# Expert loop of a hybrid-encoder kernel: each expert's turn and output products placed ahead of the next expert's up product

## The reference, cut to what matters

```python
def hier_moe(h, w_rg, b_rg, w_re, b_re, w1, w3, w2):
    ...  # combine: per token, weights of its two experts
    for gi in range(MOE_GROUPS):
        hid = silu(einsum('td,edf->tef', hf, w1[gi])) * einsum('td,edf->tef', hf, w3[gi])
        out = out + einsum('tef,efd->td', hid * combine[:, gi, :, None], w2[gi])
```

## Time and profile before

| | |
|---|---|
| median of 3 runs | 747.45 us (747.12 to 749.54) |
| the profiled execution | 747.47 us |
| its span, first to last instruction | 745.7 us |
| TensorE busy | 708.8 us (95%) |
| VectorE, ScalarE, GpSimd busy | 394.3, 266.3, 66.7 us |
| read from memory | 194.57 MB |
| granted TensorE clock, mean | 0.987 |

### The profile page before, as it was taken

The page is one execution under the profiler, slowest core; times in us unless marked ns, Lnnn a source line. Parts: engine busy times, 40 slices in busy tenths (PEclk is TensorE's granted clock), DMA queues, the critical chain, the costliest instruction groups (busy, mean ns, idle before and its releaser), DMA issues.

```text
span 745.7 us, 13196 instructions
## 1 busy us (share of the span) xinstructions
PE 708.8 (95%) x5610; PEld 568.5 (76%) x5610; DVE 394.3 (53%) x683; ACT 266.3 (36%) x378; POOL 66.7 (9%) x66
## 2 busy tenths in 40 slices
PE   9899999999999999999999999979999999988892
PEld 7689999978777777799998998866666666655442
DVE  3386867854555556997877457444422222121226
ACT  3246555446455254434436244332122112211001
POOL 0010000000000250530000000001111111111110
PEclk9999999999999999999999999999999999999997
DMA  9964756765765345333363467968999999999951
GB/s 367 416 228 170 281 182 221 278 225 213 266 249 218 130 163 172 117 114 115 114 226 121 162 226 285 422 272 321 420 415 420 419 421 420 418 421 419 419 235 56
DMA packets 30893, 200.48 MB, mean 269 GB/s; under 512 B 4999, under 2 KB 5383, under 8 KB 7410
## 3 DMA queue, kind: packets, MB, share of 16 engines
q1 hardware_dynamic: 27506, 193.01, 66.8%
q0 software_dynamic: 3328, 6.62, 2.4%
HBM read 194.57 MB, written 10.75 MB: 275 GB/s over the span
## 4 chain that ended last, share of the span: by engine, by line
PE 79%; DMA 10%; DVE 5%; ACT 2%; SPq 2%; issue 1%; DVEq 0%; ACTq 0%
PE ps L1421 77%; DMA ring<-in_expert_pieces 7%; DMA r_btm<-in_pieces 2%; SPq L420 1%; DVE ring_rounded L851 1%; PE ps L1541 1%; ACT ring_rounded L565 1%; PE ps L1828 1%; DMA ring<-in_pieces 1%; ACT r_lm L774 0%; DVE r_kq L1054 0%; DVE r_xs_rounded L1117 0%; DVE x_sb L1379 0%; DVE x_sb L1404 0%; DVE x_sb L1396 0%
## 5 line engine op out<-in xcount | busy, mean ns | idle before, releaser
L851 DVE TENSOR_TENSOR ring_rounded<-ring,ring_rounded 128x2048 fp32r<-128x2048 f32 x60 | 138.0, 2304 | 97.0 <-ACT ring_rounded L565 96.7
L1421 PE MATMUL ps<-hT_rounded,ring_rounded 128*128 128x256 f32 x832 | 154.6, 286 | 0.9 <-DVE x_sb_rounded L890 0.9
L565 ACT CAST ring_rounded<-ring 128x2048 fp32r<-128x2048 f32 x60 | 114.2, 1904 | 69.3 <-DMA ring<-in_pieces 39.7
L1421 PEld LDWEIGHTS ps<-hT_rounded,ring_rounded 128*128 128x128 f32 x832 | 131.6, 193 | 4.3 <-issue 4.2
L1421 PE MATMUL ps<-x_sb_rounded,ring_rounded 128*128 128x256 f32 x416 | 118.2, 284 | 0.0
L1421 PE MATMUL ps<-ring_rounded,hT_rounded 128*128 128x512 f32 x352 | 109.9, 393 | 0.0
L1421 PEld LDWEIGHTS ps<-x_sb_rounded,ring_rounded 128*128 128x128 f32 x416 | 80.3, 193 | 0.2 <-issue 0.2
L1421 PEld LDWEIGHTS ps<-ring_rounded,hT_rounded 128*128 128x128 f32 x352 | 65.3, 188 | 15.3 <-issue 2.2
L1421 PE MATMUL ps<-ring,r_lm 128*64 128x256 f32 x512 | 65.5, 380 | 3.2 <-DMA ring<-in_expert_pieces 3.2
L1421 PEld LDWEIGHTS ps<-ring,r_lm 128*64 128x64 f32 x512 | 42.8, 137 | 27.2 <-issue 12.5
L783 ACT ACTIVATE sq<-ps 128x128 f32<-128x128 f32 x32 | 8.9, 278 | 151.3 <-PE ps L1421 151.3
(11 more groups left out here) (298 smaller groups left out, 1106.0 us busy)
## 6 DMA issues: line engine op xcount, KB each, us to landing
ring<-in_pieces SPq DMA_DIRECT2D x76, 1024.0 KB, 5.1
ring<-in_expert_pieces SPq DMA_DIRECT2D x48, 1024.0 KB, 19.6
r_z<-in_expert_pieces SPq DMA_DIRECT2D x12, 1024.0 KB, 15.8
r_xs<-in_expert_pieces SPq DMA_DIRECT2D x12, 1024.0 KB, 17.2
g_sb<-in_expert_pieces SPq DMA_DIRECT2D x6, 1024.0 KB, 17.4
r_st<-in_expert_pieces SPq DMA_DIRECT2D x6, 1024.0 KB, 19.1
r_bt<-in_expert_pieces SPq DMA_DIRECT2D x6, 1024.0 KB, 22.7
hT<-in_expert_pieces SPq DMA_DIRECT2D x6, 1024.0 KB, 22.2
```

The costliest lines, as they stand in the source:

```text
L565: nc.scalar.copy(high_of(p_), slot_of(p_)).then_inc(hi_ok, 1)
L851: nc.vector.tensor_tensor(low_of(p_), slot_of(p_), high_of(p_).bitcast(F32), ALU.subtract).then_inc(lo_ok, 1)
L1421: return nc.tensor.matmul(o, l, r, start=start, stop=stop)
```

## The change

TensorE finishes an expert before it begins the up product of the next: up(e), select(e+5), turn(e), down(e). At e = 0 select(4) stands between up(0) and select(5). ScalarE's and VectorE's lists follow: `silu_of(e)` ahead of the rows of quarter e+5, `hidden(e)` ahead of `hidden_turned(e)`. The late experts' picks move from e = 27 to e = 28. The up product and the hidden rows of expert 29 move behind the loop. The instructions are the same ones.

```diff
 # ScalarE
             for m in range(5):
                 rows_of_quarter(m)
-            silu_of(0)
             for e in range(EARLY_E):
-                silu_of(e + 1)
+                silu_of(e)
                 if e + 5 < E:
                     rows_of_quarter(e + 5)
...
-            for e in range(EARLY_E + 1, E):
+            for e in range(EARLY_E, E):
                 silu_of(e)
...
 # VectorE
             rows_of_choices()
-            hidden(0)
             for e in range(EARLY_E):
                 if e % 4 == 2 and e // 4 + 2 < E // 4:
                     pick_quad(e // 4 + 2)
+                hidden(e)
                 hidden_turned(e)
-                hidden(e + 1)
-                if e == EARLY_E - 2:
+                if e == EARLY_E - 1:
                     picks_of_late_experts()
                 output(e)
...
+            hidden(EARLY_E)
             hidden_turned(EARLY_E)
             rows_of_late_experts()
             output(EARLY_E)
...
 # TensorE
             for m in range(4):
                 select_quarter(m)
-            up_of(0)
-            select_quarter(4)
...
             for e in range(EARLY_E):
-                up_of(e + 1)
-                turn_of(e)
+                up_of(e)
+                if e == 0:
+                    select_quarter(4)
                 if e + 5 < E:
                     select_quarter(e + 5)
+                turn_of(e)
                 down_of(e)
...
+            up_of(EARLY_E)
             turn_of(EARLY_E)
             late_rows_turned()
             down_of(EARLY_E)
```

## The result

The changed kernel takes 771.8 us (median of 4 runs, 769.28 to 773.84), the kernel before 748.35 us (4 runs, 747.12 to 749.54). The ratio is 1.0306, 95% interval 1.0275 to 1.0337: 3.1% slower. The forecast was 763.2 us, with a range of 759 to 769. The direction was right, the size was not: 23.5 us instead of 15.8. The time lies above the range, where the forecast had put 3 chances in a hundred.

The account below looks back on a forecast made before the run. TensorE bounds the loop's first half and the weight stream its second. Waits at experts 0 and 2 and turns of 7.50 us instead of 6.71, slack included, add 15.8 to 747.47: 763.2 us, range 759 to 769.

Parts of the forecast that it names:

- The bound: Expert loop: TensorE paces the first half, the weight stream the second, with 10.2 us of slack; afterwards TensorE's own waits.
- Rival A: Expert loop: the stream stays the bound and the new waits vanish in it, 748.1 or 745.8 us; chance 0.06.
- The two round trips: Each turn: select covers silu and hidden by 0.2 us; the turned rows' copy is uncovered, transpose to down 0.89 us.
- rival D: Each turn: select fails to cover silu and hidden, 0.2 us paid 26 times, 768 us; chance 0.85 together with the forecast.
- Rival C: Each turn: half the cost through overlap, for instance a turn of 7.2 us, about 755 us; chance 0.06.
- The steady turn: Experts 3 to 29: a turn with a select takes 7.50 us (terms sum to 7.51), where it took 6.71.
- up to last start 3.25, on to select 0.21: Steady turn: 3.25 us from first to last up matmul's start, then 0.21 until select starts.
- upper bound for a turn, 7.60: Steady turn: 7.60 us if hidden is ready 0.1 us later than the select's cover.
- The clock: Waits at experts 0 and 2: a drop costs about 1.6 us; none charged in the sum, up to two in the range.
- rival B: Expert loop: the clock falls in most turns, 1.6 us in each of 27, about 806 us; chance 0.03, part falls included.
- The range: Whole kernel: 759 us with 7.42 us turns and no expert 2 wait; 769 with 7.60 us turns and two clock drops.

Follow-up runs that it names:

- experiment 3: The kernel before, loading only an eighth of each down piece that goes into a used slot: 738.46 us, ratio 0.9848.
- experiment 4: The changed kernel, loading only an eighth of each down piece that goes into a used slot: 771.93 us, ratio 1.0289 to the kernel before.
- Experiment 5: The changed kernel with the turn ahead of the selection: up(e), turn(e), select(e+5), down(e): 773.86 us, ratio 1.0339 to the kernel before.
- experiment 9: The changed kernel with ScalarE's silu table loaded early and each selection from the sixth on split around the turn: 759.02 us, ratio 1.0155 to the kernel before.
- experiments 2: The changed kernel with ScalarE's silu table loaded early by one dummy activation ahead of the selections: 770.46 us, ratio 1.0271 to the kernel before.
- experiments 8: The kernel before, loading pieces 19 and 20 ahead of 18 and, from piece 50, up pieces ahead of the previous expert's down piece: 750.61 us, ratio 1.0018.
- experiments 1: The changed kernel with small dummy products filling TensorE's waits at experts 0 and 2: 768.99 us, ratio 1.0253 to the kernel before.
- 6: The kernel before, with only expert 28's turn and down moved ahead of up(29): 749.18 us, ratio 1.0001.
- 7: The kernel before, with loads of pieces 19 and 20 issued ahead of 18: 748.34 us, ratio 0.9992.

## Why the prediction was right in kind and wrong in size

**The bound, right.** The forecast read the old loop as TensorE's in its first half and the stream's in its second, with 10.2 us of slack; experiment 3 measured 10.6. It said that the new loop would use this up and be TensorE's throughout; experiment 4 shows that. Rival A is out.

**The two round trips, right.** Transpose to down is 0.88 us (582.88 to 583.76) for 0.89. The select covers silu and hidden: hidden is ready 0.44 us before the next product starts, so rival D is out. The waits were 2.07 us at expert 0 and 1.39 at expert 2, for 2.0 and 1.64 forecast. Rival C, half the cost, is out: the idle time of 0.56 us is there in all 22 turns of the row above.

**The steady turn, mis-sized: 7.50 for 7.68.** The step that failed is "up to last start 3.25, on to select 0.21", 3.46 us in all: from the first up product to the first product of the select are 3.59 (577.82 to 581.41). The 0.21 was taken from the old turn, where the up product was followed by the one-column products. The other terms are 1.14 for the select (forecast 1.12), 0.33 for the one-column products (0.27), 0.88 from transpose to down (0.89) and 1.74 from down to up (1.77). They add up to 7.68 and are 0.17 above the 7.51 of the sum; from 7.50 it is 0.18 us a turn, 4.3 us in 24 turns.

The right step could have been read from the kernel before, in two places: select(4) follows up(0) there, 3.61 us after its start (497.53 to 501.14), and the transpose of expert 28 follows up(29) by 3.61 (701.90 to 705.51). So the longer step belongs to the pair of products and not to the new order. In the old turn the weight load of the one-column products started beneath the last up matmuls:

```profile
567.81 0.48 PEld L1421 LDWEIGHTS ps<-r_btm,r_pv_rounded 128*64 128x64 f32 x8
```

The select's first load is of 128 columns and starts only at 581.40, with 0.39 us without any load ahead of it. That the width of the load is the cause is argued from these rows; no run changed it alone. Experiment 5 does not test it: there TensorE waits 0.70 us for the hidden rows at this place, longer than the step. The forecast's upper bound for a turn, 7.60, did not hold this.

**The clock, mis-sized: none charged, two falls happened.** This is the second step that failed. The forecast named both places and a price of 1.6 us each, but charged none in the sum. Measured were 3.04 us for both, 1.7 of them at expert 0. There the clock fell in each of the three profiles with 2 or 3 us of waiting, and in experiment 9 with 1.13, and not where the wait was cut to 0.65 or filled; all six profiles fit the wait as the cause there. At expert 2 it fell in one profile of five with 1.38 us or more, so there it is partly luck which execution pays it. The rule of the Trainium skill (page "TensorE: Matmul & The Clock Gate", section "A second HAM failure mode: psum-queue depth-cycling"), as rival B read it, would have let the clock alternate in the steady loop as well. There the trace disagrees: 24 turns, each with 0.56 us of idle time, ran at 1.00. Rival B is out.

**The account.** 4.3 from the turns and 3.0 from the clock are 7.3 of the 7.4 us by which the loop is longer than forecast (233.80 for 226.36); some 0.2 more came from the turns 1 and 2, and the two turns without a select took 0.1 less. With them the forecast would be 770.7 us; the measured median is 771.8.

**The range, too narrow.** It took both falls in at its upper end, with a turn of 7.60. It did not take in what the part ahead of the loop does by itself from one execution to the next, though nothing there differs between the kernels but, in experiments 2 and 9, the early table. Up(0) began at 497.53 in the profile before and at 500.29 in the one after. The clock goes with it. The same window of the two:

```profile
250.00:300.00 50.00, 48.19 (x304) 38.60 (x303) 32.70 (x46) 21.30 (x31) 17.98 (x14) 1.00 0.43 148
...
250.00:300.00 50.00, 48.53 (x278) 38.51 (x278) 29.66 (x43) 22.34 (x32) 16.34 (x12) 0.97 0.42 146
```

A clock of 0.97 over 50 us is some 1.5 us of lost time (an estimate: 3% of 50). The stretches of 50 us from 0 to 450 us show it once in the profiles before and of the experiments 8 and 9, where up(0) began at 497.5 to 497.7. They show it twice, or one 0.93 for it, in the experiments 1, 3, 6 and 7 (499.2 to 499.3), three times by this count after and in the experiments 2 and 4 (500.3 to 500.7), and four times in experiment 5 (502.2). So differences of some us between two executions of the same code can come from this alone, and a comparison of loops should start at up(0), as the table above does.

## What to carry to other kernels

When two round trips of an engine through its neighbours are to be hidden, ask for each what lies beneath it after the move: here one select of 1.1 us could not cover two round trips of 1.1 and 0.9 us, while in the old order the up product of the next expert covered the one and the select the other. When a sum is built from steps between instructions, take each step from a place where the same two instructions follow one another, since 0.13 us are 3 us over a loop. And a wait of 1 to 2 us can cost 1.3 to 1.7 us more by the clock that it lets fall: put that into the sum with its chance, and not only into the range.

## What the runs showed of the hardware

The same waits let the clock fall in one execution and not in another: 1.39 us before turn(2) and 0.56 before down(2) were followed by 0.50 in the profile after, and by 1.00 in experiment 4; with 1.38 and 0.56 it stayed at 1.00 in experiment 2, and even 2.53 us ahead of turn(2) in experiment 5 and 1.86 in experiment 9, with no wait behind them, left down(2) at full speed (1.94 us). And in experiment 9 a wait of 1.13 us with 24 one-column products behind it was enough. The length of a wait alone does not decide it. A fall cost 1.7 us at expert 0 and 1.3 at expert 2.

A weight load of 64 columns started beneath the last matmuls of the up product, and one of 128 columns only 0.39 us behind the loads ahead of it. The product behind it started 3.59 to 3.61 us after the up product did, instead of 3.46.
